# The end of a two-layer trunk kernel: the last expert's 80 rows are handled apart from the sum of the other fifteen

## What is computed

```
def expert_choice_ffn(h, w_router, w_gate, w_up, w_down):
    cap = EC_FACTOR * n // N_EXPERTS          # 64 sample rows, 16 prompt rows for each of 16 experts
    aff = jax.nn.softmax((xt @ w_router).astype(jnp.float32), axis=-1)
    gate, idx = lax.top_k(aff.T, cap)
    xe = jnp.take(xt, idx, axis=0)
    hid = jax.nn.silu(xe @ w_gate) * (xe @ w_up)
    ye = (hid @ w_down) * gate
    y = jnp.zeros_like(xt).at[idx.reshape(-1)].add(ye.reshape(-1, D))

x = x + gate2 * expert_choice_ffn(h2, ...)
y_prompt, y_sample = rmsnorm(xp, g_final), rmsnorm(xs, g_final)    # over 1024 values of each row
```

## Time and profile before

| what | value |
|---|---|
| median of three runs | 3097.07 us (3097.04 to 3099.41) |
| the profiled execution's own time | 3095.03 us |
| its span in the trace | 3093.1 us |
| PE busy | 3021.7 us, 98% of the span |
| DVE, ACT, POOL busy | 1239.7, 607.4, 234.6 us |
| moved by DMA | 695.55 MB, mean 225 GB/s |

### The profile page before, as it was taken

The page is one execution under the profiler, slowest core; times in us unless marked ns, Lnnn a source line. Parts: engine busy times, 40 slices in busy tenths (PEclk is TensorE's granted clock), DMA queues, the critical chain, the costliest instruction groups (busy, mean ns, idle before and its releaser), DMA issues.

```text
span 3093.1 us, 49605 instructions
## 1 busy us (share of the span) xinstructions
PE 3021.7 (98%) x21914; PEld 1609.3 (52%) x21914; DVE 1239.7 (40%) x2404; ACT 607.4 (20%) x1349; POOL 234.6 (8%) x374
## 2 busy tenths in 40 slices
PE   7999999999999999999999999999999999999998
PEld 3555565656556444444455546666565464444443
DVE  4459553364354121221254694532643442122113
ACT  3241001144423100000032400011534230000001
POOL 0011000021001000000100100000110010000000
PEclk9999999999999999999999999999999999999999
DMA  6235442432343999999941552433223349999997
GB/s 269 95 130 194 149 150 92 151 110 74 133 156 118 383 397 395 402 396 397 380 191 55 189 198 90 150 127 134 92 74 143 143 142 408 396 407 399 395 404 286
DMA packets 102295, 695.55 MB, mean 225 GB/s; under 512 B 11787, under 2 KB 25143, under 8 KB 66753
## 3 DMA queue, kind: packets, MB, share of 16 engines
q1 hardware_dynamic: 75296, 613.97, 50.3%
q0 software_dynamic: 20736, 62.80, 6.9%
q10 hardware_dynamic: 6048, 15.62, 1.3%
HBM read 618.66 MB, written 73.68 MB: 224 GB/s over the span
## 4 chain that ended last, share of the span: by engine, by line
PE 84%; DMA 12%; ACT 2%; DVE 1%; issue 0%; POOL 0%; ACTq 0%; DVEq 0%; POOLq 0%
PE unit L994 14%; PE unit L948 12%; PE unit L1513 10%; DMA xT<-in_w_e_gate 9%; PE work L1516 8%; PE work L1513 5%; PE unit L1006 4%; PE unit L985 4%; PE unit L1025 4%; PE unit L1369 4%; PE unit L938 3%; PE work L962 1%; PE work L1168 1%; DMA ring<-in_w_ada 1%; PE unit L1381 1%; PE work L1191 1%
## 5 line engine op out<-in xcount | busy, mean ns | idle before, releaser
L994 PE MATMUL unit<-hT,ring 128*128 128x512 f32 x1024 | 452.6, 595 | 0.0
L994 PEld LDWEIGHTS unit<-hT,ring 128*128 128x128 f32 x1024 | 189.4, 190 | 217.7 <-issue 217.7
L2539 DVE SCALAR_TENSOR_TENSOR arena<-work,arena 32x256 f32<-32x256 f32 x128 | 61.7, 482 | 541.7 <-PE work L1516 540.3
L1513 PE MATMUL unit<-ring,arena 128*32 128x512 f32 x2112 | 239.0, 593 | 0.6 <-DVE arena L2527 0.6
L948 PE MATMUL unit<-hT,ring 128*128 128x512 f32 x512 | 222.2, 592 | 0.0
L1516 PE MATMUL work<-ring,arena 128*32 128x256 f32 x3072 | 183.8, 380 | 0.4 <-DVE arena L2527 0.4
L2009 ACT ACTIVATE arena<-work 128x512 f32<-128x512 f32 x32 | 19.1, 598 | 822.1 <-PE work L1531 822.1
L1623 ACT ACTIVATE xT<-unit 128x512 f32<-128x512 f32 x92 | 54.9, 596 | 590.5 <-PE unit L994 384.7
L948 PE MATMUL unit<-arena,ring 128*128 128x512 f32 x384 | 167.9, 593 | 1.6 <-ACT arena L1623 0.9
L948 PEld LDWEIGHTS unit<-hT,ring 128*128 128x128 f32 x512 | 96.2, 190 | 115.8 <-issue 115.3
L1516 PEld LDWEIGHTS work<-ring,arena 128*32 128x32 f32 x3072 | 97.3, 110 | 90.4 <-issue 37.8
(11 more groups left out here) (443 smaller groups left out, 4221.6 us busy)
## 6 DMA issues: line engine op xcount, KB each, us to landing
ring<-in_w_e_up SPq DMA_DIRECT2D x64, 2048.0 KB, 25.3
ring<-in_w_in SPq DMA_DIRECT2D x32, 2048.0 KB, 12.8
arena<-in_w_e_gate SPq DMA_DIRECT2D x32, 2048.0 KB, 24.3
arena<-in_w_e_down SPq DMA_DIRECT2D x32, 2048.0 KB, 25.8
xT<-in_w_e_gate SPq DMA_DIRECT2D x30, 2048.0 KB, 25.8
ring<-in_w_e_down SPq DMA_DIRECT2D x30, 2048.0 KB, 26.2
ring<-in_w_ada SPq DMA_DIRECT2D x24, 2048.0 KB, 9.3
spill<-xT SPq DMA_DIRECT2D x94, 256.0 KB, 9.7
```

Of the source, the lines that this page charges most:

```text
L994: last = mm(bank[:, :], w[:, k, m * P:(m + 1) * P], hT[:, k, 0:TS], start=k == 0, stop=k == KD - 1)
L1513: last = mm(big[SLOTP * c:SLOTP * c + SLOTP, :], x[:, s0:s0 + SLOTP], w[:, kk, 512 * (c // 2):512 * (c // 2) + 512], start=k == 0, stop=k ...
L2539: STT(y[SLS:SLS + SLOTP, 256 * c:256 * c + 256], W[5][r, 0:256], gpro[r, e:e + 1], gatep[r, :], ALU.mult, ALU.mult)
```

## The change

Instead of adding the last expert to all 640 rows before the norm, the kernel norms and stores the sum of fifteen experts for all rows. The 80 rows of the last expert are read a second time from `moesum`, get the expert's result added, are normed by themselves, and overwrite their rows in the outputs.

```
@@ gpsimd, after the five loads of L906
+            pool.indirect_dma_start(late_rows[0:SL, :], None, moesum[DEPTH - 1],
+                                    bass.IndirectOffsetOnAxis(token[:, NE - 1:NE], 0)).then_inc(sig["late_rows_loaded"], 16)
+            pool.wait_ge(sig["y_ready"], NT + 1)
+            pool.wait_ge(sig["x_moved"], 16 * (2 * DEPTH + NT))
+            pool.indirect_dma_start(O["y_sample"][0], bass.IndirectOffsetOnAxis(token[0:SLS, NE - 1:NE], 0),
+                                    late_rows[0:SLS, :], None).then_inc(sig["late_rows_loaded"], 16)
+            pool.indirect_dma_start(O["y_prompt"][0], bass.IndirectOffsetOnAxis(last_prompt, 0),
+                                    late_rows[SLS:SL, :], None).then_inc(sig["late_rows_loaded"], 16)
+            pool.wait_ge(sig["late_rows_loaded"], 48)
@@ tensor: the ten products with onehot (L1587 to L1599) are gone
@@ scalar
+            act.wait_ge(sig["scattered"], 16 * SUMS * DEPTH)
             for t in range(NT):
-                act.wait_ge(sig["x_added"], LAST_ADDS + t + 1)
                 ch.link(a_(ysq, ysum[t], ACT.Square, accum_out=orms[:, t:t + 1]))
                 a_(orms[:, t:t + 1], orms[:, t:t + 1], ACT.Sqrt, bias=eps, scale=1.0 / D)\
                     .then_inc(sig["tokens_rooted"], 1)
+            for half in range(2):
+                act.wait_ge(sig["x_added"], LAST_ADDS + half + 1)
+                a_(ysq[0:SL, 512 * half:512 * half + 512], late_rows[0:SL, 512 * half:512 * half + 512], ACT.Square,
+                   accum_out=orms[0:SL, NT + half:NT + half + 1]).then_inc(sig["tile_squared"], 1)
+            act.wait_ge(sig["tile_squared"], (H + 2) * DEPTH + 2)
+            act.wait_ge(sig["x_added"], LAST_ADDS + 3)
+            a_(orms[0:SL, NT + 1:NT + 2], orms[0:SL, NT + 1:NT + 2], ACT.Sqrt, bias=orms[0:SL, NT:NT + 1], scale=1.0 / D)\
+                .then_inc(sig["tokens_rooted"], 1)
@@ vector, in the routing step of each layer (made in the last one alone)
+                if l + 1 == DEPTH:
+                    TSC(last_prompt, W[3][0:SLP, P + 2 * NE - 1:P + 2 * NE], -float(TS), None, ALU.add)
@@ vector, at the end
-            dve.wait_ge(sig["scattered"], 16 * SUMS * DEPTH)
+            copy_rows(NE - 1)
+            final = Y[(NE - 1) % NROWS]
+            dve.wait_ge(sig["left_copied"], NE * DEPTH)
+            dve.wait_ge(sig["right_copied"], NE * DEPTH)
+            dve.wait_ge(sig["late_rows_loaded"], 16)
+            for half in range(2):
+                x = late_rows[0:SL, 512 * half:512 * half + 512]
+                TT(x, x, final[0:SL, 512 * half:512 * half + 512], ALU.add).then_inc(sig["x_added"], 1)
             for t in range(NT):
-                for half, bank in enumerate(last_banks(t)):
-                    dve.wait_ge(sig["sum_turned"], (KD + 2) * (DEPTH - 1) + 2 * t + half + 1)
-                    x = ysum[t][:, 512 * half:512 * half + 512]
-                    last = TT(x, bank[:, :], x, ALU.add)
-                last.then_inc(sig["x_added"], 1)
-                if t:
-                    finish(t - 1)
-            finish(NT - 1)
+                finish(t)
+            dve.wait_ge(sig["tile_squared"], (H + 2) * DEPTH + 1)
+            TSC(orms[0:SL, NT:NT + 1], orms[0:SL, NT:NT + 1], 1.0 / D, EPS, ALU.mult, ALU.add).then_inc(sig["x_added"], 1)
+            dve.wait_ge(sig["tokens_rooted"], 2 * DEPTH + NT + 1)
+            ch.link(v_.reciprocal(orms[0:SL, NT + 1:NT + 2], orms[0:SL, NT + 1:NT + 2]))
+            STT(late_rows[0:SL, :], late_rows[0:SL, :], orms[0:SL, NT + 1:NT + 2], frow[0:SL, :], ALU.mult, ALU.mult)\
+                .then_inc(sig["y_ready"], 1)
```

More of the change, by code:

```diff
@@ L482, in build @@
         frow = at(10496, (D,))
-        ysq = at(NS, (D,))
+        tflat = hT.rearrange("p k t -> p (k t)")
+        ysq, late_rows = tflat[:, 0:D], tflat[:, D:2 * D]
         cond = at(5120, (2, KD))
@@ L553, in build @@
         rank, token = slotu[0:NE, 0:SL], slotu[0:SL, SL:SL + NE]
-        first_prompt = slotu[0:SLP, 0:1]
+        first_prompt, last_prompt = slotu[0:SLP, 0:1], slotu[0:SLP, 1:2]
         block = ctx.enter_context(nc.Block())
@@ L1587, in _ @@
                     pass
[L1589 to L1599, removed]
         @block.scalar
@@ L2553, in _ @@
                 for e in range(NE + 1):
-                    if e:
+                    if e and (e < NE or l + 1 < DEPTH):
                         copy_rows(e - 1)
```

## The result

| kernel | median | runs |
|---|---|---|
| before | 3097.69 us | 20, 3092.04 to 3103.22 |
| changed | 3105.63 us | 20, 3101.33 to 3114.22 |

The changed kernel takes 1.0028 times as long (95% interval 1.0022 to 1.0035): slower by 7.9 us between the medians. The forecast was 3095.1, 2.0 us faster, with a range up to 3101.0. It was wrong, in direction and in size.

What follows compares the result with a forecast made beforehand. PE bounds the kernel (98% busy), so only the 20.3 us tail changes: last tile 7.3 us sooner, 5.3 returned to the second stores, -2.0 us off the median 3097.07 gives 3095.1; range 3091.5 to 3101.0.

Steps and rivals of the forecast that it cites:

- ACT's first square: ACT, at the end: started by the landing of the sums at 3072.3 instead of by DVE's adds at 3076.37.
- gather of the late rows landed ahead of the end of `copy_rows`: POOL's second reading of 80 rows: lands at 3073.2, before DVE ends the copy at 3074.36, costing nothing; cover 1.2 us.
- DVE's late adds begin: DVE, after the copy: two adds of 80x512 run from 3074.4 to 3075.7, some 1.3 us back to back.
- spacing of the multiplies: DVE, five tiles: reciprocal and multiply set a period of 1.39 us, slower than ACT's 1.36.
- last tile's store issued: SP, fifth tile: store issued at 3082.76, 10 us behind PE's end and not 17.3, landing at 3085.36.
- POOL from the landing to the indirect issue: POOL, after SP's last store lands: its first indirect store begins 0.81 us later, at 3086.2.
- first to second issue: POOL, two indirect stores: an issue costs 0.88 to 1.43 plus 0.30 to the next, so the second starts at 3087.7.
- second store, issue to landing: POOL's last indirect store: 1.2 us of issue plus 1.8 of flight, as for a plain store, 3.0 in all, landing at 3090.7.
- from the last landing to the end: End of the span: 0.42 us after the last landing, as in the kernel before, giving 3091.1.
- rival B: Late-row gather lands at 3079.8 and holds DVE's adds, moving everything behind by 5.4 us to 3100.5, slower; chance 0.08.
- rival A: Final indirect stores land like adding scatters in 10.7 us, span end 3099.1, +6.0, time 3103.0, slower; chance 0.14.
- The four rivals: Slow-landing indirect stores 0.14, late gather 0.08, cheaper end at 3093.5 (0.70 together with the forecast), upstream variation of some 2 us 0.08.

Runs made afterwards that it cites:

- e4: Changed kernel without its two indirect stores and GpSimd's waits behind them, late rows normed but not stored; median 3090.27 us, ratio 0.9978 to before.
- e3: Changed kernel with SP instead of GpSimd waiting for the two indirect stores to land; median 3103.49 us, ratio 1.0020 to before.
- e8: Small kernel without the computation, GpSimd issues no DMA and waits last for SP's last store; 0.4 us from landing to end, span's end 29.5.
- e1: Kernel before, with GpSimd waiting at the end of its list for SP's last store, no DMA added; ratio 1.0033 to before, tail 29.8 us.
- e2: Kernel before, with GpSimd waiting at the end of its list until the fourth tile is ready; ratio 1.0013 to before, tail 25.4 us.
- e7: Kernel before, with GpSimd waiting at the end of its list until the first tile is ready; ratio 1.0002 to before, tail 20.4 us.

## Why the prediction was wrong

Counted from PE's last projection, step by step:

| step | predicted | measured |
|---|---|---|
| ACT's first square | -0.5 | 3074.84, -1.5 |
| gather of the late rows landed ahead of the end of `copy_rows` | by 1.2 | 3067.28 + 8.2 = 3075.5, by 2.4 |
| DVE's late adds begin | 1.6 | 3078.38, 2.0 |
| spacing of the multiplies | 1.39 | 1.39 |
| last tile's store issued | 10.0 | 3086.67, 10.3 |
| POOL from the landing to the indirect issue | 0.81 | 3089.31 to 3090.20, 0.89 |
| first to second issue | 1.5 | 1.26 |
| second store, issue to landing | 3.0 | 2.8 |
| last landing | 17.9 | 17.9 |
| from the last landing to the end | 0.42 | 9.9 |
| tail | 18.3 | 27.9 |

**What held.** All steps on the path up to the last landing came out within half a microsecond. That their sum fits to a tenth is in part luck: DVE began its adds 0.4 late, and the shorter issue (1.26 for 1.5) and flight (2.8 for 3.0) took it back. The adds' 6.4 us and the hidden table load were gained; e4 gives the tail without the stores as 13.4, where the steps of the prediction make 3085.36 + 0.42 - 3072.8 = 13.0. The gather was hidden (rival B fell: it landed in 8.2 us), but 1.6 of the 2.4 us of cover are the slow clock's, which held PE back while the loads went on. e3 has no such stretch there, and shows the order that the prediction priced (POOL and DVE in order of time):

```profile
3064.73 0.96 POOL L909 DMA_INDIRECT hT<-moe_sum,slotu  x1 [0.30 <-issue]
```
```profile
3071.95 1.53 DVE L2552 SCALAR_TENSOR_TENSOR arena<-work,arena 64x512 f32<-64x512 f32 x2 [1.41 <-PE work L1523]
3073.92 1.29 DVE L2597 TENSOR_TENSOR hT<-hT,arena 80x512 f32<-80x512 f32 x2 [0.44 <-DVE arena L2552]
```

There the gather landed 8.0 us after its issue, at 3072.7, only 0.8 ahead of the end of `copy_rows` at 3073.5, and ACT began at 3071.95, 0.1 behind PE's end and not 1.5 ahead. The 0.44 us between `copy_rows` and the adds, which the prediction put at nearly nothing, stand behind DVE's own copies, by the releaser in e3's row. The indirect stores landed like plain ones and not like the adding scatters (rival A fell: 3.3 and 2.8 us, for 10.7). The fixed cost and the rate that the Trainium skill gives for a DMA issued by GpSimd (DMA: Bandwidth & Descriptors, "Anatomy of one DMA — SWDGE (gpsimd) path") make an estimated 2.15 us of the 64 KB store. The trace has 2.8 from the start of its issue and 2.8 - 0.86 = 1.9 from the end of it.

**What failed** is the last term of the sum, "0.42 to the span's end". I read it from the earlier trace rows, where SP's store was the last event, and carried it over to a kernel in which GpSimd's was. It was what remains when GpSimd has been through for long (or, as e8 shows, has issued no DMA). The 9.8 us of GpSimd would have run in the kernel before from 3065.2 on, beside other engines' work, and no view shows an instruction for them. e1 and e2 price them (9.8, twice), e7 shows their cover, e3 shows them in the changed kernel (9.7) and e4 shows it without them on the path. With them the forecast of the difference would have been -2.0 + 9.8 - 0.4 = +7.4, for 7.9 measured. The four rivals all looked for the loss inside the traced work. None asked what an engine still has to do when its list is through, though the prediction itself put GpSimd's stores last.

The range went with it: its upper end of 3101.0 came from B, and slower by over 0.2% had a chance of 0.07, for the sake of A. Its spread between runs, 2.4 us from three runs, was small as well: the twenty runs of before reach from 3092.04 to 3103.22.

## What to carry over

When a change makes another engine the last one, the stretch between last landing and end isn't to be carried over: ask what ends with that engine. In a kernel like this one, in which GpSimd has issued about 300 DMAs, its last wait should be satisfied some 10 us ahead of the end. A wait 12.5 us ahead was free, and later ones moved the end by their full lateness. Moving the final wait from GpSimd to SP is a one-line edit, worth 2 us in the trace here. A single pair of profiles can differ by microseconds ahead of the changed part (here 3.5, of which the granted clock makes some 3.2), so count from a common event and leave the total to the timed runs.

## What was not expected of the hardware

- From GpSimd's last wait to the end of the span 0.4 us pass if it has issued no DMA, 4.4 after 160 plain loads, 8.3 after 320, 3.1 after 160 indirect gathers and 9.8 after the 288 mixed ones of this kernel.
- A plain indirect store of 64 rows of 4 KB lands 3.3 us after its issue began and one of 16 rows 2.8, where the adding scatter of 80 rows takes 10.7 (median) beside weight loads.
- The granted clock of TensorE fell to the 1.2 GHz level for about 3 us at 3064 in the changed kernel's profile, after a gap that left it at 2.4 GHz in the other, and cost PE 1.6 us.
